# The last two experts' rows placed by 0/1 matrices, and the next weights loaded between the rows

## The reference, cut to what matters

```python
# each token picks 2 of 32 experts; comb are its two weights
yb = (silu(x_blk @ w1[e]) * (x_blk @ w3[e])) @ w2[e]      # rows of expert e
out[token] += yb * comb                                     # two rows per token
x = x + out
x = rmsnorm(x, norm_final_g)                                # end of block one
h = rmsnorm(x, ln_a)
b_gate, c_gate, u, z = split(h @ w_in_a, 4)                 # start of block two
```

## Time and profile before

| | us |
|---|---|
| median of 3 runs (lowest, highest) | 1485.23 (1479.86, 1485.5) |
| the profiled execution | 1482.86 |
| its span | 1481.0 |
| TensorE busy | 1339.9 (90%) |
| VectorE busy | 538.2 (36%) |
| ScalarE busy | 414.5 (28%) |
| GpSimd busy | 389.1 (26%) |

### The profile page before, as it was taken

How to read it: one execution, slowest core, us unless ns; L and a number is a source line. 1 busy time by engine, 2 the same in 40 slices (tenths; PEclk the granted TensorE clock), 3 DMA queues, 4 the chain that set the end, 5 groups by cost and what they waited for, 6 DMA issues and landing times. The chain is left out here.

```text
span 1481.0 us, 16780 instructions
## 1 busy us (share of the span) xinstructions
PE 1339.9 (90%) x6344; PEld 892.0 (60%) x6344; DVE 538.2 (36%) x1074; ACT 414.5 (28%) x810; POOL 389.1 (26%) x372
## 2 busy tenths in 40 slices
PE   7999998999999799888888788866999999999799
PEld 6777766898758633333222223325888887788467
DVE  3649947430242511111111111127321414563753
ACT  5333365163331100000000000024223224343641
POOL 7553223168320112111111111100445440000321
PEclk9999988999999899999999999998999999999999
DMA  7221221244205879999999999983222322222000
GB/s 210 74 98 58 93 79 45 102 167 142 85 5 212 366 310 420 420 424 420 424 422 421 423 423 421 423 318 136 96 104 85 114 86 85 86 86 86 29 22 36
DMA packets 72368, 298.27 MB, mean 201 GB/s; under 512 B 10168, under 2 KB 10216, under 8 KB 51568
## 3 DMA queue, kind: packets, MB, share of 16 engines
q1 hardware_dynamic: 64848, 282.80, 48.7%
q0 software_dynamic: 7456, 14.59, 3.1%
HBM read 293.16 MB, written 12.58 MB: 206 GB/s over the span
## 5 line engine op out<-in xcount | busy, mean ns | idle before, releaser
L748 POOL TENSOR_TENSOR ring_rounded<-ring,ring_rounded 128x512 fp32r<-128x512 f32 x192 | 251.5, 1346 | 350.0 <-ACT ring_rounded L1463 350.0
L875 PE MATMUL bank<-HT_rounded,ring_rounded 128*128 128x512 f32 (+1 forms) x576 | 220.9, 383 | 4.4 <-DVE ring_rounded L2358 3.5
L877 PE MATMUL bank<-HT_rounded,ring_rounded 128*128 128x512 f32 (+1 forms) x576 | 217.5, 378 | 0.0
L876 PE MATMUL bank<-ring_rounded 128*128 128x512 f32 (+1 forms) x576 | 217.4, 377 | 0.0
L1176 PE MATMUL bank<-ring,B 128*64 128x512 f32 x704 | 170.3, 633 | 43.2 <-DMA ring<-in_w 42.3
L2250 DVE TENSOR_TENSOR B<-bank,small 128x512 f32<-128x512 f32 x32 | 22.1, 692 | 325.4 <-PE bank L1166 325.4
L1176 PEld LDWEIGHTS bank<-ring,B 128*64 128x64 f32 x704 | 52.1, 144 | 145.3 <-issue 105.0
L877 PE MATMUL bank<-ring_rounded 128*128 128x512 f32 x352 | 137.7, 391 | 0.0
L1463 ACT ACTIVATE ring_rounded<-ring 128x2048 fp32r<-128x2048 f32 x54 | 102.8, 1915 | 108.8 <-DMA ring<-in_w_in_a 46.3
L875 PEld LDWEIGHTS bank<-HT_rounded,ring_rounded 128*128 128x128 f32 x576 | 108.3, 188 | 31.1 <-issue 6.0
L876 PEld LDWEIGHTS bank<-ring_rounded 128*128 128x128 f32 x576 | 108.4, 188 | 20.3 <-issue 1.0
(11 more groups left out here) (382 smaller groups left out, 1988.1 us busy)
## 6 DMA issues: line engine op xcount, KB each, us to landing
ring<-in_w SPq DMA_DIRECT2D x88, 1024.0 KB, 30.2
A<-in_w SPq DMA_DIRECT2D x21, 2048.0 KB, 28.6
ring<-in_w SPq DMA_DIRECT2D x11, 2048.0 KB, 28.6
XN<-in_w SPq DMA_DIRECT2D x20, 1024.0 KB, 29.1
HT<-in_w SPq DMA_DIRECT2D x20, 1024.0 KB, 32.2
ring<-in_w_in_a SPq DMA_DIRECT2D x16, 1024.0 KB, 5.0
ring<-in_w_in SPq DMA_DIRECT2D x14, 1024.0 KB, 7.0
ring<-in_w_in_b SPq DMA_DIRECT2D x8, 1024.0 KB, 5.3
```

Of the source, the lines that this page charges most:

```text
L748: last = pool.tensor_tensor(r32(lo), lo, r32_read(quarter(g, True)[:, k, :]), ALU.subtract)
L875: pe.matmul(o, r32(a_hi), r32(b_hi), start=first, stop=False)
L876: pe.matmul(o, r32(a_hi), r32(b_lo), start=False, stop=False)
L877: return pe.matmul(o, r32(a_lo), r32(b_hi), start=False, stop=last)
```

## The change

The results of experts 30 and 31 are no longer scattered. `down_last` puts the left halves of both experts' columns in bank 6 and the right halves in bank 7: expert 30 in partitions 0 to 63 of bank 6 and 64 to 127 of bank 7, expert 31 the other way round. VectorE weighs bank 6 and ScalarE bank 7, into `y_last`. For each half VectorE builds a 0/1 matrix `last_oh[b]` of 128 rows (the slots of the two experts) by 512 columns (tokens). `last_rows(t)` multiplies 128 of its columns by the rows in `y_last`, which puts each row at its token, in a bank; `add_last(t)` adds the bank to the residual. For tile 2 the two parts of `y_back` are added in the same bank, by two matmuls with the identity, and `add_back(2)` is gone. Rows of `y_dram` that only the last two experts would have written must now be zero: SyncE writes zeros to the whole of `y_dram` behind the fourth chunk's loads of the first block.

SyncE's reads of `y_dram` wait for the scatters up to expert 29 and for the `down` of expert 30. The norm gains go to `A1`. `c0`'s two halves are loaded after tiles 0 and 1 and the gains, in front of tiles 2 and 3; `u0` after tile 3. `c0`'s first 256 tokens are multiplied by the high part in a first run over the four banks and by the low part in a second. VectorE makes the low part of `c0` after `scale_final(2)`, ScalarE the high part between its sums for tiles 0 and 1.

```diff
-    first = [(("x4_t", t, b), "dve") for t in range(NT) for b in range(2)]
+    rows = lambda name, t: [((name, t, b), "dve") for b in range(2)]
+    first = rows("last", 0) + rows("last", 1) + rows("last", 2) + rows("x4_t", 0) + rows("x4_t", 1)
+    first += rows("last", 3) + rows("x4_t", 2) + rows("x4_t", 3)
...
-    opened = closed[0:4] + [("c", j) for j in range(4)] + closed[4:8] + closed[12:]
+    opened = closed[0:12] + [("c", j) for j in range(4)] + closed[12:16] + closed[20:]
...
+        PAIR = EXPERTS - 2
...
+        y_over = B2[:, 1536:2048]
+        y_last = E[:, 1024:2048]
+        last_scale, last_at, last_at2, blocks = B2[:, 160:162], B2[:, 162:164], B2[:, 164:166], B2[:, 168:176]
+        last_oh = [B2[:, 512:1024], B2[:, 1024:1536]]
...
-        g_fin, g_a_row = B0[:, 0:D], B0[:, D:2 * D]
+        g_fin, g_a_row = A1[:, 0:D], A1[:, D:2 * D]
+        x3_squares = f3(A1, (2, D), 2 * D)
...
+                if c == 3:
+                    sp.wait_ge(sem("zeros_ready"), 1)
+                    for q in range(4):
+                        sp.dma_start(y_dram[SEQ * q:SEQ * q + SEQ, :].rearrange("(p r) n -> p r n", p=P),
+                                     y_over.unsqueeze(1).to_broadcast([P, 4, 512])).then_inc(sem("y_zeroed"), 16)
...
-            for n, c in enumerate(("c0", "u0")):
-                sp.wait_ge(h_done, EXPERTS - 1 + n)
-                for h in range(2):
-                    load_half(2 * chunk_no[c] + h)
...
-            sp.wait_ge(sem("pe_left_experts"), 1)
+            sp.wait_ge(y_done, EXPERTS - 1)
...
+                    sp.wait_ge(h_done, EXPERTS - 1)
+                    for h in range(2):
+                        load_half(2 * chunk_no["c0"] + h)
+
+            sp.wait_ge(h_done, EXPERTS)
+            for h in range(2):
+                load_half(2 * chunk_no["u0"] + h)
...
-            for e in range(24, EXPERTS):
+            for e in range(24, PAIR):
                 step_rows(e, e)
             for b in range(2):
-                pool.wait_ge(sem(f"y_stored{b}"), 16 * EXPERTS // 2)
+                pool.wait_ge(sem(f"y_stored{b}"), 16 * PAIR // 2)
...
+            def down_last(j, n):
+
+                pe.wait_ge(sem("gT_ready"), PAIR + j + 1)
+                pe.wait_ge(we_loaded[n % 3][2], 16 * ((PAIR + j) // 3 + 1))
+                pe.wait_ge(sem("y_ready"), PAIR)
+                w = as_expert(w_slot[n % 3][2], 2).rearrange("p (k n) -> p k n", k=4)
+                for k in range(4):
+                    for hf in range(2):
+                        at = 64 * ((hf + j) % 2)
+                        last = pe.matmul(bank[6 + hf][at:at + 64, :], gT[n % 2][:, k, :],
+                                         w[:, k, 512 * hf:512 * hf + 512], start=(k == 0), stop=(k == 3),
+                                         skip_group_check=True)
+                last.then_inc(y_done, 1)
...
-            step_down(4, 6)
+            wait_emptied(pe, U["table",])
+            n_over = pe.value_load(over_n, min_val=0, max_val=OVER)
+            down_last(0, 6)
             step(4, 7)
-            step_down(4, 7)
+            down_last(1, 7)
             pe.wait_ge(sem("y_ready"), EXPERTS)
-
-            wait_emptied(pe, U["table",])
-            n = pe.value_load(over_n, min_val=0, max_val=OVER)
-            with pe.If(n > 0):
+            pe.wait_ge(sem("y_last_ready"), 1)
+
+            with pe.If(n_over > 0):
...
+            def last_rows(t):
+
+                for b in range(2):
+                    o = fill(V, "last", t, b)[:, :]
+                    cs = slice(512 * b, 512 * b + 512)
+                    if t == 2:
+                        pe.wait_ge(sem("y_back2"), 32)
+                        for c in range(2):
+                            pe.matmul(o, ident, y_back[t][:, c, cs], start=(c == 0), stop=False)
+                    pe.matmul(o, last_oh[b][:, P * t:P * t + P], y_last[:, cs], start=(t != 2), stop=True)\
+                      .then_inc(bank_filled, 1)
...
-                    if t == 0 and b == 0:
-                        pe.wait_ge(sem("x3_ready"), 1)
-                        spin(o, 9)
+                    if t == 1 and b == 0:
+                        spin(o, 4)
...
+            for t in range(3):
+                last_rows(t)
             turn_x4(0)
             turn_x4(1)
+            last_rows(3)
             outs = [fill(V, "c", j) for j in range(4)]
-            part = chunk("c0")
-            spin(outs[0], 4)
-            for h in range(2):
-                wait_emptied(pe, V["x4_t", 2 * h + 1, 1])
-                at = slice(2 * P * h, 2 * P * h + 2 * P)
-                for j, o in enumerate(outs):
-                    for k in range(KD):
-                        last = passes(o[:, at], lambda k: part(k, P * j, P * j + P),
-                                      lambda k: (hT[:, k, at], lowT[:, k, at]), k, k == 0, k == KD - 1)
-                    if h == 1:
-                        last.then_inc(bank_filled, 1)
-                    elif j % 2 == 1:
-                        turn_x4(2 + j // 2)
+            part = weights(chunk_no["c0"])
+            spin(outs[0], 3)
+            pe.wait_ge(w_high_ready, 2 * chunk_no["c0"])
+            wait_emptied(pe, V["x4_t", 1, 1])
+            at = slice(0, 2 * P)
+            for j, o in enumerate(outs):
+                for k in range(KD):
+                    hi = part(k, P * j, P * j + P)[0]
+                    pe.matmul(o[:, at], r32(hi), r32(hT[:, k, at]), start=(k == 0), stop=False)
+                    pe.matmul(o[:, at], r32(hi), r32(lowT[:, k, at]), start=False, stop=False)
+            wait_split(pe, chunk_no["c0"], 1)
+            for j, o in enumerate(outs):
+                for k in range(KD):
+                    lo = part(k, P * j, P * j + P)[1]
+                    pe.matmul(o[:, at], r32(lo), r32(hT[:, k, at]), start=False, stop=(k == KD - 1))
+                if j % 2 == 1:
+                    turn_x4(2 + j // 2)
+            wait_emptied(pe, V["x4_t", 3, 1])
+            at = slice(2 * P, 4 * P)
+            for j, o in enumerate(outs):
+                for k in range(KD):
+                    last = passes(o[:, at], lambda k: part(k, P * j, P * j + P),
+                                  lambda k: (hT[:, k, at], lowT[:, k, at]), k, k == 0, k == KD - 1)
+                last.then_inc(bank_filled, 1)
...
+            act.wait_ge(sem("y_stored1"), 16 * PAIR // 2)
+            act.wait_ge(sem("last_oh_ready"), 2)
+            act.activation(y_last[:, 512:1024], bank[7][:, :], ACT.Copy, scale=last_scale[:, 1:2])\
+               .then_inc(sem("y_last_ready"), 1)
...
-            high_parts("c0", "u0")
...
-            square_x3(0)
-            square_x3(1)
             for t in range(2):
+                high_half("c0", t)
+                square_x3(t)
                 square_x3g(t)
                 roots(16 + 2 * t, 18 + 2 * t)
             high_x4(0)
             high_x4(1)
             square_x3(2)
             square_x3g(2)
+            high_parts("u0")
             square_x3(3)
-            roots(20, 22)
             square_x3g(3)
-            roots(22, 24)
-            high_x4(2)
-            high_x4(3)
+            for t in (2, 3):
+                roots(16 + 2 * t, 18 + 2 * t)
+                high_x4(t)
...
-            pair(EXPERTS // 2 - 1, False, True)
-            step_weigh(EXPERTS // 2 - 1, 1)
+            step_cols(PAIR // 2, 1)
+            step_gate(PAIR // 2, 0)
+            step_weigh(PAIR // 2 - 1, 1)
+
+            for b in range(2):
+                top, bottom = PAIR + b, PAIR + 1 - b
+                dve.tensor_copy(last_scale[0:SLOTS, b:b + 1], tab_w[0:SLOTS, top:top + 1])
+                dve.tensor_copy(last_scale[SLOTS:P, b:b + 1], tab_w[SLOTS:P, bottom:bottom + 1])
+                dve.tensor_copy(last_at[0:SLOTS, b:b + 1], tab_s[0:SLOTS, top:top + 1])
+                last = dve.tensor_copy(last_at[SLOTS:P, b:b + 1], tab_s[SLOTS:P, bottom:bottom + 1])
+            own(last)
+            own(dve.tensor_scalar(blocks, const("item_row")[:, 0:TILES], float(SLOTS), None, ALU.mult))
+            own(dve.tensor_tensor(last_at, last_at, const("half_col").to_broadcast([P, 2]), ALU.subtract))
+            dve.tensor_scalar(last_at2, last_at, -float(SEQ), None, ALU.add)
+            own(dve.tensor_tensor(f3(B2, (TILES, SLOTS), 1536),
+                                  const("slot_row")[:, 0:SLOTS].unsqueeze(1).to_broadcast([P, TILES, SLOTS]),
+                                  blocks.unsqueeze(2).to_broadcast([P, TILES, SLOTS]), ALU.add))
+            row_no = y_over
+            for b, oh in enumerate(last_oh):
+                own(dve.tensor_scalar(oh, row_no, last_at[:, b:b + 1], None, ALU.is_equal))
+                dve.scalar_tensor_tensor(oh, row_no, last_at2[:, b:b + 1], oh, ALU.is_equal, ALU.add)\
+                   .then_inc(sem("last_oh_ready"), 1)
+
+            step_gate(PAIR // 2, 1)
+            dve.wait_ge(sem("y_done"), EXPERTS)
+            for b in range(2):
```

(14 more changed lines are left out.)

73 lines of the change are left out of this document (46 added, 27 removed).

## The result

The changed kernel takes 1488.62 us (median of 20 runs, 1483.55 to 1492.92), the kernel before 1484.24 (median of 20, timed beside it; one of these runs, at 2661.72, is an outlier). The ratio is 1.0034, 95% interval 1.0024 to 1.0044: some 5 us slower, which is less than 0.5%. The profiled execution took 1490.71 us, its span 1488.6, 7.6 more than before's.

The account below looks back on a forecast made before the run. Bound: TensorE nearly full, except before `c0`'s second half, which waits for VectorE's chain behind rows from `y_dram`. That start moves +1.5 us: 1482.9 to 1484.4 profiled, median 2.4 above, 1486.7, stated as 1486; range 1480 to 1493.

Parts of the forecast that it names:

- What goes: After the last expert: without two scatters the first read is 13.8 us earlier, VectorE starts at 993.1, gross gain 9.5 us.
- Hidden work: 0: Table building, some 6 us, hides in VectorE's idle time before expert 31's gate product; TensorE's count read also costs 0.
- The added wait: Before `last_rows(2)`: TensorE waits for `y_back2`, which lands at 1004.2, with 5.3 us for `c0`'s loads queued ahead.
- `last_rows(2)` at the low clock: Its six calls take 5.4 us plus 2.1 lost to the lower clock, 7.5 us, until 1011.7.
- First part: Up to the end of `low_x4(1)` on VectorE: reached at 1017.1 in place of 1020.5, 3.4 us earlier.
- Second part: From `low_x4(1)`'s end to `c0`'s second half: 20.8 us in place of 15.9, so that half starts 1.5 us later.
- After that both programs are alike.: From the start of `c0`'s second half on, the change makes no further difference.
- (c): Rival: TensorE's added waits between `c0`'s halves bring the lower clock; second half loses 2.1 us, 1488 us; chance 0.07.
- (a): Rival: transfers land earlier, `y_back2` at 1000 or before; `c0`'s second half starts 4 us earlier, 1481 us; chance 0.20.
- (b): Rival: `y_back2` lands 6 us later than counted, at 1010; +7.5 us, 1494 us; chance 0.13.
- (d): Rival: early in block one, writing the zeros delays the fourth chunk by 5 us, 1491 us; chance 0.05.
- (e): Rival: TensorE reaches `c0` no earlier because `c0`'s two low halves still hold it; called excluded, no chance given.

Follow-up runs that it names:

- e9: The changed kernel run once more, unaltered, for its profile; one run without a ratio, 65.4 us from the last expert's down projection's start to `u0`.
- e2: The changed kernel with `c0`'s two loads issued ahead of all the rows, as in the kernel before; ratio 1.0005 to the kernel before.
- e5: The changed kernel with filler sized to the waits: 14 calls before `last_rows(2)`, then 5, 4 and 3 between `c0`'s halves; ratio 0.9999 to the kernel before.
- e6: The changed kernel with `normalise_x4(3)` ahead of `low_x4(2)` on VectorE and both roots ahead of `high_x4(2)` on ScalarE; ratio 1.0019 to the kernel before.
- e3: The changed kernel with `c0`'s low parts computed by GpSimd in place of VectorE; ratio 1.0023 to the kernel before.
- e7: e2 with `c0`'s high parts on ScalarE and its first low part on VectorE ahead of the last expert's products; ratio 1.0000 to the kernel before.
- e10: The kernel before run once more, unaltered, for its profile; one run without a ratio, 61.7 us from the last expert's down projection's start to `u0`.
- e1: The kernel before with only the change's 4 MB of zeros written to `y_dram` added; 1483.31 us against 1483.1, ratio 1.0003.
- e4: The changed kernel with too much filler: 30 calls before `last_rows(2)`, then 9, 7 and 5 between `c0`'s halves; ratio 1.0056 to the kernel before.
- e12: The changed kernel with only the later part of e5's filler: 5, 4 and 3 calls between `c0`'s halves; ratio 1.0016 to the kernel before.
- e8: e7 with e6's order and filler of 6 calls before `last_rows(2)` and 3 before `c0`'s second half; 1475.9 us against 1482.8, ratio 0.9951.
- e11: The changed kernel with only the first part of e5's filler: 14 calls before `last_rows(2)`; ratio 1.0006 to the kernel before.

## Why the prediction was right, and where it was short

It said 1486 (own range 1483 to 1490, all 1480 to 1493) and "within 0.5%"; 1488.6 is inside both. The range was wide enough to hold no change at all, and the size was missed: the sum was +1.5 us, measured were about +5. That the number came within 2.6 is in part luck, since it was counted from a median of 1485.23 and the kernel before, timed beside the changed one, took 1484.24. From D to C the first profiles differ by 5.2 us: the 1.5 forecast, 0.9 in the first part, 1.3 in the second and 1.5 behind it. Step by step, from D where the moment matters:

- **What goes.** First read predicted at 984.0, measured 985.20 with D 1.4 later: right. VectorE's start, predicted 5.5 after D, measured 4.9: right. The gross gain of 9.5 us is there (10.0 from D), and more than used up.
- **Hidden work: 0.** `down_last(0)`, with TensorE's read of the count ahead of it, started 0.47 after ScalarE as the down projection did before, and D to the last product is 3.8 against 3.7: right.
- **The added wait.** `y_back2` predicted 16.6 after D, measured 16.7 (e9 too). That `c0` in the queue costs its transfer is shown by e2 (13.8, so 2.9 us and not the 5.3 I counted: ahead of the reads `c0` moves partly in the same time as they).
- **`last_rows(2)` at the low clock.** Predicted 7.5, measured 8.0 and 7.4. That the clock does it is shown by e5: 5.4.
- **First part.** Predicted 3.4 earlier than before, measured 2.5 and 3.1.
- **Second part.** Predicted 20.8 us from A to B. Measured 22.1 and 21.4; the low parts (4.48) and `add_last(3)` (1.28) as priced, the idle time 5.1 us in place of the 3.4 summed. The 1.7 more: 0.84 since a turn and its rounding leave VectorE idle for 1.57 and not 1.15, 0.54 for two roots of 0.27 that I had left out, 0.54 for `turn_x4(3)` at the low clock, less 0.23 at the first root. e6 gives back 2.2 of it.
- **"After that both programs are alike."** This is the step that failed: what comes behind the start of `c0`'s second half was put at nothing and took 1.5 us more. It rested on rival (c) being unlikely (0.07), since before's wait of 1.64 us in front of 1036.43 had not brought the clock down. But before has only one more wait there (0.40, at 1027.02), while the changed kernel waits 2.61, 2.00 and 1.48 us between the halves, and 2.60, 0.65 and 1.63 in e9. I had written these waits down and given them too little weight. From B to C the clock was low in both profiles of the changed kernel and in e2, e3 and e7. It was not low there in the three profiles without the placing (before, e10, e1), nor with filler between the halves (e4, e5, e12, e8), nor in e6 and e11. The price of (c) was near: 2.1 us, measured 1.5 from B to C and 0.5 before it. That the total came to its 1488 is in part chance, since the parts before B were short as well. The granted clock of 0.50 from 1040 to 1044 agrees with what the Trainium skill's page TensorE: Matmul & The Clock Gate, section HAM oscillation, says of a TensorE kept waiting between short bursts, which I had set below that one row; the waits that it tells of are longer than these, and e6, which waits 2.60 and 1.64 us, does not follow it.
- **What makes the clock fall stays open.** In the first profile it fell behind the second wait, in e9, e2 and e11 already behind the first, of 2.60 us, with TensorE busy up to it. In e6 the same wait of 2.60 left it at 1.00. And in the kernel before (e10) it fell at 1020, behind waits of 2.42 and 1.04. So neither one wait nor several together decide it in these traces; shown is that with the added waits it came between the halves or behind them in six of the seven profiles that have the placing and no filler there, and that it came in none of the four with filler there (in e8 the filler stands before B alone, and e6's order had taken out the middle wait).
- **(a), (b), (d), (e).** No early landing; `y_back2` at 1005.7, below the 1008 from which (b) decides; (d) shown to be nothing by e1.

So two things are each shown to be worth most of the 5 us by taking them away: where `c0`'s loads stand (e2: 1.0005), and the low clock in two places (e5: 0.9999). They overlap, since what delays the rows also lengthens TensorE's wait. The order of tiles 2 and 3 on VectorE (e6) and `c0`'s low part in its chain (e3) count as well by the profiles, and all four gains together exceed the loss. They are ways to win it back and not parts that add up to it. e8 has the placing with `c0` ahead of the rows, its low part in a wait and tile 3's order as the kernel before had them, and the clock kept: 7.3 us faster. How much of that is the placing alone was not separated.

## What to carry over

A chain that starts 9 us earlier is worth only what the same engines don't get added to it: list the additions on that chain first, and then the waits that they leave on TensorE. Waits of 2 us and more between short pieces of work can bring the low clock; one row without it is no proof, since the same wait of 2.60 us went both ways here. A load of weights that has a gap in the queue before the round trip's answer should be issued before it; put between the rows, it delays them. Filler must be sized by the row (0.44 to 0.47 us a call here), or it holds up what it should warm.
